# The order of halves and high/low products in the dense products of a two-layer hybrid encoder step

## The reference, cut to what matters

```python
def swiglu(u, w_up, w_down):
    gate, val = jnp.split(u @ w_up, 2, axis=-1)
    return (jax.nn.silu(gate) * val) @ w_down

def layer_forward(x, p_i, pos, past, w, lb):
    h = x + 0.5 * swiglu(rmsnorm(x, w['ffn1_norm']), w['ffn1_up'], w['ffn1_down'])
    a = rmsnorm(h, w['mix_norm']) @ w['w_in']
    ...
    h = h + jnp.concatenate([o_mla, o_swa, o_hg], axis=-1) @ w['w_out']
    h = h + 0.5 * swiglu(rmsnorm(h, w['ffn2_norm']), w['ffn2_up'], w['ffn2_down'])
    gate = jax.nn.sigmoid(rmsnorm(h, w['ple_norm']) @ w['ple_gate'])
    h = h + gate * (p_i @ w['ple_proj'])
```

## Time and profile before

| | us |
|---|---|
| median of 3 runs | 2846.82 |
| the three runs | 2846.82, 2845.34, 2863.1 |
| span of the profiled execution (first to last instruction) | 2841.2 |
| its own whole time | not recorded beside the span |
| PE busy | 2749.4 |
| DVE busy | 1343.7 |
| ACT busy | 780.5 |
| mean granted clock of TensorE | 0.928 |

### The profile page before, as it was taken

One profiled execution on the slowest core, in us unless ns is written; L12 is line 12 of the kernel. 1 busy time (PEld: TensorE's weight loads), 2 busy tenths in 40 slices (PEclk: granted clock), 3 DMA queues, 4 the chain that ended last, 5 costly groups with the idle time before them and its releaser, 6 DMA issues. The chain is left out here.

```text
span 2841.2 us, 48671 instructions
## 1 busy us (share of the span) xinstructions
PE 2749.4 (97%) x19056; PEld 2570.2 (90%) x19056; DVE 1343.7 (47%) x1944; ACT 780.5 (27%) x1221; POOL 265.2 (9%) x153
## 2 busy tenths in 40 slices
PE   6999999998999999999999999999989999999997
PEld 5999999986568999999999999999755699999996
DVE  5434345556534543434653343455764345343357
ACT  3212123212433322222232222332133322222232
POOL 3000003000002100002400000210000040000043
PEclk9999999965679999999999999999558799999998
DMA  3322222110001222222223222222000022222232
GB/s 133 107 83 81 82 82 96 60 49 1 1 1 45 82 82 82 82 81 96 82 76 109 81 88 78 93 75 74 20 1 1 1 75 80 84 81 82 81 97 78
DMA packets 58399, 196.15 MB, mean 69 GB/s; under 512 B 8785, under 2 KB 10962, under 8 KB 58130
## 3 DMA queue, kind: packets, MB, share of 16 engines
q1 hardware_dynamic: 56816, 190.60, 20.5%
q10 hardware_dynamic: 1442, 3.61, 0.4%
HBM read 190.30 MB, written 3.88 MB: 68 GB/s over the span
## 5 line engine op out<-in xcount | busy, mean ns | idle before, releaser
L1246 PE MATMUL ps<-xg_hi,w_hi 128*128 128x288 f32 x3520 | 758.2, 297 | 32.9 <-DVE w_lo L705 28.4
L1246 PE MATMUL ps<-xg_lo,w_hi 128*128 128x288 f32 x3520 | 755.4, 296 | 0.0
L1246 PE MATMUL ps<-xg_hi,w_lo 128*128 128x288 f32 x3520 | 755.3, 296 | 0.0
L1246 PEld LDWEIGHTS ps<-xg_hi,w_hi 128*128 128x128 f32 x3520 | 569.4, 189 | 35.2 <-issue 28.8
L1246 PEld LDWEIGHTS ps<-xg_hi,w_lo 128*128 128x128 f32 x3520 | 569.0, 189 | 0.0
L1246 PEld LDWEIGHTS ps<-xg_lo,w_hi 128*128 128x128 f32 x3520 | 568.9, 189 | 0.0
L705 DVE TENSOR_TENSOR w_lo<-w_raw,w_hi 128x1024 fp32r<-128x1024 f32 x347 | 436.4, 1258 | 230.7 <-ACT w_hi L456 226.0
L456 ACT ACTIVATE w_hi<-w_raw 128x1024 fp32r<-128x1024 f32 x347 | 364.0, 1050 | 523.6 <-PE ps L1246 464.0
L1246 PE MATMUL ps<-hid_hi,w_hi 128*128 128x288 f32 x1664 | 356.4, 296 | 0.0
L1246 PE MATMUL ps<-hid_lo,w_hi 128*128 128x288 f32 x1664 | 356.4, 296 | 0.0
L1246 PE MATMUL ps<-hid_hi,w_lo 128*128 128x288 f32 x1664 | 356.3, 296 | 0.0
(11 more groups left out here) (211 smaller groups left out, 2516.5 us busy)
## 6 DMA issues: line engine op xcount, KB each, us to landing
w_raw<-w_all SPq DMA_DIRECT2D x347, 512.0 KB, 3.4
h<-x_t ACTq DMA_DIRECT2D x1, 2304.0 KB, 9.5
y_t<-y SPq DMA_DIRECT2D x8, 288.0 KB, 2.3
uq_w<-uq SPq DMA_DIRECT2D x2, 768.0 KB, 4.7
p_raw<-p_t SPq DMA_DIRECT2D x2, 576.0 KB, 6.7
ukv_w<-ukv SPq DMA_DIRECT2D x2, 384.0 KB, 3.1
ckv<-ckv_c SPq DMA_DIRECT2D x2, 256.0 KB, 4.9
ckv_o<-ckv SPq DMA_DIRECT2D x2, 256.0 KB, 2.1
```

Source lines behind the costliest of these rows:

```text
L1246: ins = pe.matmul(ps[:, bank(u) + c, 0:HALF], w, m[:, k, c * HALF:(c + 1) * HALF], start=(k == kts[0] and i == 0), stop=(k == kts[-1] and ...
```

## The change

In `dense` the loop over the halves c goes outside the loop over the three products i; both stay inside the loop over k. The slice of the half gets a name. The matmuls, their operands, their banks and their `start` and `stop` flags are the same.

```diff
@@ -1241,9 +1241,10 @@
                     if wait is not None:
                         wait(k)
                     wh, wl = (w[:, s, w_at(k):w_at(k) + P] for w in (w_hi, w_lo))
-                    for i, (w, m) in enumerate(((wh, src_hi), (wh, src_lo), (wl, src_hi))):
-                        for c in range(2):
-                            ins = pe.matmul(ps[:, bank(u) + c, 0:HALF], w, m[:, k, c * HALF:(c + 1) * HALF],
+                    for c in range(2):
+                        cols = slice(c * HALF, (c + 1) * HALF)
+                        for i, (w, m) in enumerate(((wh, src_hi), (wh, src_lo), (wl, src_hi))):
+                            ins = pe.matmul(ps[:, bank(u) + c, 0:HALF], w, m[:, k, cols],
                                             start=(k == kts[0] and i == 0), stop=(k == kts[-1] and i == 2))
```

## The result

The changed kernel takes 2862.84 us (median of 11 runs, 2859.07 to 2877.79), the kernel before 2845.22 us (11 runs, 2840.22 to 2863.1). The ratio is 1.0067, with a 95% interval of 1.0045 to 1.0089: 0.7% slower. It is 17.6 us over the kernel before, 16.0 us over the forecast of 2846.8 us, and 0.8 us outside the range of 2838 to 2862 us.

The account below looks back on a forecast made before the run. TensorE's matmul pitch in the dense products was taken as the bound. Added instructions, bank order, weight order and waits each came to 0, so 2846.8 + 0 = 2846.8 us, range 2838 to 2862 us.

Parts of the forecast that it names:

- What bounds the kernel, and that nothing is added to the dense products: Dense products at L1246: TensorE's pitch of 133.3 ns bounds, 2,099 us or 74% of the span; matmuls and loads unchanged, 0.
- The bank term: Dense products: 10,496 transitions go from other bank to same bank; taken as 0, with ends 64 us faster and 65 us slower.
- rival A: Dense products: a change of bank costs 6.1 ns, so the new order is 64 us faster, 2783 us; chance 0.08.
- rival B: Second and third matmul of each half: staying in a bank stalls, up to 65 us slower, 2912 us; chance 0.05.
- the prediction's 122.5 ns: Dense matmul of 288 columns: the formula N / 2.4 + 2.5 ns, against 133.3 ns in the trace.
- The bounds: Ends for the bank changes, 64 us faster to 65 us slower, from an estimated bare pass of 121 ns for 288 columns.
- One pitch for all 15,744 matmuls: Dense products: 133.3 ns from the window 100 to 200 us, applied to every matmul, giving 2,099 us.
- "Sum: 0": Whole kernel: all changes and waits add 0, so 2846.8 + 0 = 2846.8 us; no change has chance 0.85.
- The order of the weights: Dense products: fresh weight blocks per k turn go from 2 to 4, 5,248 more in all; taken as 0.
- rival C: Dense products: each fresh weight block costs 10 ns, so 52 us slower, 2899 us; chance 0.02.
- What would show it: Dense products: about 753 matmuls in 100 to 200 us, 19,056 loads, and the longer step still after every fourth matmul.
- The range: Whole kernel: 2838 to 2862 us, from three earlier runs at 2845.3 to 2863.1 us; leaves out the rivals (0.15).

Follow-up runs that it names:

- the same pad: Six repeated matmuls of ones ahead of the mix norm of each layer: 2852.97 us on the old order, 2851.89 us on the new order.
- run 17: Not a run number: the words are "a run 17 us above the other two", one of three runs of the unchanged kernel before, 2863.1 us.
- the kernel with three filled units: New order with two extra matmuls of the unit matrix ahead of the transposes of units 48 to 50 of each layer's attention: 2846.97 us.

## Why the prediction was wrong, point by point

- *What bounds the kernel, and that nothing is added to the dense products.* Right, at the place looked at: 753 matmuls in the window of 100 us before and 752 after, 133.3 ns each.
- *The bank term, 0 between -64 and +65 us.* Right as a price in the steady pace. With the same pad the two orders lie 1.1 us apart. So "a change of bank costs" (rival A) and "staying in a bank stalls" (rival B) are both off; what was tested is how often the bank changes. The Trainium skill's advice to use all 8 banks ("Perfetto Trace Analysis", "Matmul Optimizations") was not tested: both orders use all eight, so it doesn't speak against this change, though the prediction says so. The formula behind the prediction's 122.5 ns is what the Trainium skill ("TensorE: Matmul & The Clock Gate", "Back-to-back issue gap") gives for a matmul by itself; this stream has 133.3 ns. The bounds took half a record at L1260 as one bare pass, which no row ahead of the prediction shows; 240 ns for 288 columns at 1.2 GHz (below) fits it.
- *One pitch for all 15,744 matmuls.* This step was a little off. It multiplied the pitch of one window by the count of the whole kernel, though gates 4 to 7 of each layer ran at 130.0 ns. The new order loses that: 2 x 0.64 = 1.3 us.
- *"Sum: 0", so the time stays.* This is the step that failed. It took the granted clock of every stretch as a property of the kernel. The sum of the changed instructions was right within 2 us. But layer 2's attention stands 0.17 us later against the rise of the clock (3.54 instead of 3.37 us), on the other side of an edge that the table places between 3.39 and 3.45 us, and 16 us in the attention and 2.3 us in the output products at 1.2 GHz followed. The source found for the shift is the 0.64 us at the end of layer 1. That a delay with no reorder does the same, and that a larger pad takes it back, is shown. That 0.64 us is all of the shift is not: with everything else reordered, half the runs were on the upper levels, and layer 1's attention, which comes ahead of the gates, already stands 0.08 us later (3.38 instead of 3.30 us).
- *The order of the weights (rival C, +52 us).* Off, as its rows said.
- *What would show it.* The longer distance of every fourth matmul was forecast to stay; instead it is gone. In the new order the distances are 133 to 134 ns throughout, as these rows show, with the same sum:

```profile
199.77 0.29 PE L1247 MATMUL ps<-xg_hi,w_hi 128*128 128x288 f32 x1
199.90 0.29 PE L1247 MATMUL ps<-xg_lo,w_hi 128*128 128x288 f32 x1
200.03 0.29 PE L1247 MATMUL ps<-xg_hi,w_lo 128*128 128x288 f32 x1
200.17 0.30 PE L1247 MATMUL ps<-xg_hi,w_hi 128*128 128x288 f32 x1
```

- *The range.* The three runs of before that were shown already held 2863.1 us, a run 17 us above the other two. It was read as noise of the measurement; its time is that of the level on which the changed kernel lies.

## What to carry to other kernels

Where a trace shows the granted clock at both levels inside a stage, the time of an unchanged stage is not fixed: here an attention that began 0.1 to 0.2 us later against the clock took 16 us more. Before a small difference is put down to an edit, look at the granted clock window by window in both traces, and pad both kernels by the same small amounts, more than one size. If the difference goes or changes sign with a pad, and the windows show the clock's stretches come or go with it, it belongs to the clock. Runs that lie in separate levels (2843, 2861, 2877 us) rather than in one cloud are the sign that it is worth looking.

## What the runs showed of the hardware that was not expected

- The levels. Most runs of the kernels before and after lie near 2843, 2861 and 2877 us, 16 to 18 us apart (one of before lies at 2869.0 us), and the profiled runs tie the second level to one further stretch of 41 to 44 us at 1.2 GHz. The third has no profile.
- At 1.2 GHz the dense matmul takes 240 ns from start to start (0.48 us for a pair), which is 288 columns at that clock and nothing more; at 2.4 GHz it takes 133.3 ns, not 120. The low clock costs 107 ns a matmul, less than the pitch itself. Rows of the timeline before, while the clock is low at the start of layer 2:

```profile
1429.68 0.68 PE L1246 MATMUL ps<-xg_lo,w_hi 128*128 128x288 f32 x2
1430.16 0.68 PE L1246 MATMUL ps<-xg_hi,w_lo 128*128 128x288 f32 x2
```

- The same stream of matmuls has two paces, 133.3 and 130.0 ns, and holds one over several chunks. A single short matmul can set it, in the old order only as far as tried. It also begins with none near: in the run with the delay ahead of the last gate, 471 matmuls in a row from 2299.8 us on run at 130.0 ns, 0.1 us after the clock's rise at 2299.7 us. Why is open.
- What in the attention decides the fall at the edge is open too. That denser work just ahead of it prevents it is a guess that the kernel with three filled units allows and doesn't show.
